# The last two down chunks in sets of 256 tokens, and a first transfer of 256 weight columns

## The reference, cut to what matters

```python
# start: layer 0 of the first block
h = rmsnorm(x, norm_g)                     # x (1, 512, 1024)
proj = jnp.einsum("bsd,de->bse", h, w_in)
...
# end: layer 1 of the second block
h = rms_norm(x, g_ffn[l])
x = x + jnp.square(jax.nn.relu(h @ w_ff1[l])) @ w_ff2[l]   # "up", then "down"
return rms_norm(x, g_final)
```

## Time and profile before

| | us |
|---|---|
| median of 3 runs | 1961.37 |
| the profiled execution, its own time | 1961.14 |
| its span | 1959.3 |
| TensorE busy | 1928.9 (98%) |
| VectorE busy | 1145.9 (58%) |
| GpSimd busy | 1013.0 (52%) |
| ScalarE busy | 768.7 (39%) |

### The profile page before, as it was taken

One profiled execution on the slowest core, in us unless ns is written; L12 is line 12 of the kernel. 1 busy time (PEld: TensorE's weight loads), 2 busy tenths in 40 slices (PEclk: granted clock), 3 DMA queues, 4 the chain that ended last, 5 costly groups with the idle time before them and its releaser, 6 DMA issues.

```text
span 1959.3 us, 24980 instructions
## 1 busy us (share of the span) xinstructions
PE 1928.9 (98%) x9110; PEld 1600.3 (82%) x9110; DVE 1145.9 (58%) x2009; ACT 768.7 (39%) x1142; POOL 1013.0 (52%) x1273
## 2 busy tenths in 40 slices
PE   9999999999999999999999999999999999999998
PEld 7788788888788887888888888888878888888887
DVE  7986778968867667463232325666676553332335
ACT  6444544445335455323232323344554233223232
POOL 6343374342733346665654646533447566464644
PEclk9999999999999999999999999999999999999999
DMA  5222222221321213222322232222222222323231
GB/s 200 80 76 75 69 93 88 83 85 50 113 86 65 86 65 108 99 96 86 114 86 108 86 108 86 86 86 87 86 75 98 99 96 86 108 86 108 86 108 65
DMA packets 29657, 178.92 MB, mean 91 GB/s; under 512 B 3936, under 2 KB 6112, under 8 KB 9184
## 3 DMA queue, kind: packets, MB, share of 16 engines
q1 hardware_dynamic: 27376, 173.42, 24.9%
q10 hardware_dynamic: 2160, 3.91, 0.7%
HBM read 175.22 MB, written 2.10 MB: 91 GB/s over the span
## 4 chain that ended last, share of the span: by engine, by line
PE 73%; DVE 14%; issue 6%; ACT 4%; POOL 2%; DMA 0%; SPq 0%; ACTq 0%; DVEq 0%; POOLq 0%
PE bank L584 67%; POOL W_lo L550 2%; PE bank L605 2%; DVE bank L1947 2%; DVE PR L1866 1%; DVE PT_lo L1759 1%; PE bank L635 1%; DVE Y_lo L1759 1%; ACT W_hi L1235 1%; PE bank L647 1%; ACT PR L1269 1%; ACT PT_hi L1239 1%; DVE PR L1887 1%; PE bank L846 1%; DVE K_lo L1759 0%
## 5 line engine op out<-in xcount | busy, mean ns | idle before, releaser
L550 POOL TENSOR_TENSOR W_lo<-W_raw,W_hi 128x256 fp32r<-128x256 f32 (+1 forms) x1228 | 986.9, 840 | 908.8 <-ACT W_hi L1235 908.8
L584 PE MATMUL bank<-H_hi,W_hi 128*128 128x512 f32 x1264 | 500.5, 396 | 2.8 <-POOL W_lo L550 1.0
L584 PE MATMUL bank<-H_hi,W_lo 128*128 128x512 f32 x1264 | 493.3, 390 | 0.0
L584 PE MATMUL bank<-H_lo,W_hi 128*128 128x512 f32 x1264 | 492.5, 390 | 0.0
L584 PE MATMUL bank<-Y_hi,W_hi 128*128 128x512 f32 (+1 forms) x980 | 384.9, 393 | 5.6 <-DVE Y_lo L1759 3.1
L584 PE MATMUL bank<-Y_hi,W_lo 128*128 128x512 f32 (+1 forms) x980 | 380.9, 389 | 0.0
L584 PE MATMUL bank<-Y_lo,W_hi 128*128 128x512 f32 (+1 forms) x980 | 380.7, 389 | 0.0
L1235 ACT ACTIVATE W_hi<-W_raw 128x2048 fp32r<-128x2048 f32 (+2 forms) x159 | 295.8, 1863 | 202.9 <-DMA W_raw<-in_stream 198.3
L584 PEld LDWEIGHTS bank<-H_hi,W_hi 128*128 128x128 f32 x1264 | 237.9, 188 | 52.0 <-DVE Y_lo L2329 1.8
L584 PEld LDWEIGHTS bank<-H_hi,W_lo 128*128 128x128 f32 x1264 | 237.5, 188 | 50.9
L584 PEld LDWEIGHTS bank<-H_lo,W_hi 128*128 128x128 f32 x1264 | 238.1, 188 | 47.4
(11 more groups left out here) (321 smaller groups left out, 2324.1 us busy)
## 6 DMA issues: line engine op xcount, KB each, us to landing
W_raw<-in_stream SPq DMA_DIRECT2D x159, 1024.0 KB, 4.8
out<-GT SPq DMA_DIRECT2D x8, 256.0 KB, 2.5
BT<-in_bias ACTq DMA_DIRECT2D x6, 320.0 KB, 3.0
X<-in_x SPq DMA_DIRECT2D x3, 512.0 KB, 7.5
W_raw<-in_stream SPq DMA_DIRECT2D x4, 256.0 KB, 7.2
BT<-in_rope ACTq DMA_DIRECT2D x2, 512.0 KB, 3.6
BT<-in_bias SPq DMA_DIRECT2D x2, 320.0 KB, 12.6
X<-in_x SPq DMA_DIRECT2D x2, 256.0 KB, 4.2
```

What stands on the lines that cost most here:

```text
L550: ins = nc.gpsimd.tensor_tensor(W[1][:, s, part], W_raw[:, s, part], W[0][:, s, part].bitcast(F32), ALU.subtract)
L584: mm = pe.matmul(out, lhs[a], rhs[b], start=(not begun and k == 0 and a == 0 and b == 0), stop=(not more and k == n - 1 and a == 1), skip_ ...
```

## The change

**At the end.** `down` now stops at d5 for PE and DVE. Chunks d6 and d7 are both done in sets of 256 tokens (`last_part`), in the order d6 set 0, d7 set 0, five of eight weight tiles of d6 set 1, the sums of set 0, the rest of d6 set 1, four tiles of d7 set 1, the spreads of set 0, the rest of d7 set 1, and then the sums and spreads of set 1. DVE handles each of the four pieces by `last_piece`, between them the inverse and two of the final multiplications of set 0. SP sends the piece of POOL second instead of fourth in set 0.

**At the start.** The weight pieces of unit 0 are now 256, 256, 512, 512 and 512 columns. The first of them goes out ahead of the gains and of X, and ACT makes its `W_hi` before it touches X.

The core of the diff:

```diff
+FIRST_PARTS = [slice(0, 256), slice(256, 512), slice(512, 1024), slice(1024, 1536), slice(1536, 2048)]
...
+    def half_bank(t, h):
+        return ((G[0], SC[0]), (G[1], TB[0]))[t - 6][h]
...
     @block.sync
+        first_weights(0)
         sp.dma_start(PARF[:, :], dram["gains"]).then_inc(gains_in, 16)
         sp.dma_start(X[:, 0, :], dram["x"][:, 0, :]).then_inc(x_first, 16)
-        for k in range(4):
...
+        first_weights(1)
+        sp.dma_start(X[:, 1, :], dram["x"][:, 1, :]).then_inc(x_in[0], 16)
+        for k in range(1, 4):
+            sp.dma_start(X[:, 2 * k:2 * k + 2, :], dram["x"][:, 2 * k:2 * k + 2, :]).then_inc(x_in[k], 16)
+            first_weights(k + 1)
...
-        for piece in ((0, 0), (0, 1), (0, 2), (0, 3), (1, 0), (1, 1), (1, 2), (1, 3)):
+        for piece in ((0, 0), (0, 3), (0, 1), (0, 2), (1, 0), (1, 1), (1, 2), (1, 3)):
...
     @block.gpsimd
-                    pool.wait_ge(w_half, kt // 2 + 1)
+                    pool.wait_ge(w_half, kt + 1 if kt < 2 else kt // 2 + 2)
...
     @block.tensor
-                    elif seg == "f3" and l + 1 == DEPTH and n == KT - 1:
-                        for h in range(2):
-                            part = [(w, [x[:, token_half(h)] for x in data]) for w, data in pairs]
-                            three(pe, (G[1], SC[0])[h][:, token_half(h)], part).then_inc(bf.half.sem, 1)
+                    elif seg == "f3" and l + 1 == DEPTH and n >= KT - 2:
+                        last_pairs.append(pairs)
...
+        def last_part(t, h, lo, hi):
+            part = [(w, [x[:, token_half(h)] for x in data]) for w, data in last_pairs[t - 6][lo:hi]]
+            mm = three(pe, half_bank(t, h)[:, token_half(h)], part, begun=lo > 0, more=hi < KT)
+            if hi == KT:
+                mm.then_inc(bf.half.sem, 1)
...
+        last_part(6, 0, 0, KT)
+        last_part(7, 0, 0, KT)
+        last_part(6, 1, 0, 5)
+        last_sums(0)
+        last_part(6, 1, 5, KT)
+        last_part(7, 1, 0, 4)
+        last_spreads(0)
+        last_part(7, 1, 4, KT)
+        last_sums(1)
+        last_spreads(1)
...
     @block.scalar
+        last_tile(6, 0)
         act.wait_ge(*own.last(0))
         nc.scalar.activation(spare_a[:, :], ones[:, 0:1], ACT.Sqrt).then_inc(act_step, own.step())
-        last_tile(0)
+        last_tile(7, 0)
         last_root(0)
-        last_tile(1)
+        last_tile(6, 1)
         copy_factors(0)
+        last_tile(7, 1)
         last_root(1)
         copy_factors(1)
...
     @block.vector
-                for n in range(KT - 1 if after and l + 1 == DEPTH else KT):
+                for n in range(KT - 2 if after and l + 1 == DEPTH else KT):
...
+        last_piece(6, 0)
+        last_piece(7, 0)
         last_inverse(0)
+        last_piece(6, 1)
         final_norm(0, 0)
+        last_piece(7, 1)
         final_norm(0, 1)
         last_inverse(1)
         final_norm(0, 2)
```

More of the change, by code:

```diff
@@ L227, in _build @@
     x_first = sem("x_first")
-    w_part = [sem(f"w_part{k}") for k in range(4)]
+    w_part = [sem(f"w_part{k}") for k in range(5)]
     start = sem("start")
@@ L342, in _build @@
     halves = ["0", "1"]
-    bf.half = Count(sem("last_half_done"), 0, [("", 1, halves)])
-    bf.x = Count(sem("last_half_added"), 0, [("", 1, halves)])
+    pieces = ["60", "70", "61", "71"]
+    bf.half = Count(sem("last_half_done"), 0, [("", 1, pieces)])
+    bf.x = Count(sem("last_half_added"), 0, [("", 1, pieces)])
     bf.sq = Count(sem("last_half_squares"), 0, [("", 1, halves)])
@@ L351, in _build @@
     bf.rs = Count(sem("norm_copiedF"), 0, [("", 1, halves)])
-    bf.xg = Count(sem("gain_times_xF"), 0, [("", 1, [str(k) for k in range(KT - 1)] + ["70", "71"])])
+    bf.xg = Count(sem("gain_times_xF"), 0, [("", 1, [str(k) for k in range(KT - 2)] + pieces)])
     final = Count(sem("final"), 0, [("", 1, ["00", "01", "02", "10", "11", "12"])])
@@ L500, in _, with first_weights @@
     def _(sp):
+        def first_weights(k):
+            part = FIRST_PARTS[k]
+            sp.dma_start(W_raw[:, 0, part], dram["stream"][0][:, part]).then_inc(w_part[k], 16)
+        first_weights(0)
         sp.dma_start(PARF[:, :], dram["gains"]).then_inc(gains_in, 16)
         sp.dma_start(X[:, 0, :], dram["x"][:, 0, :]).then_inc(x_first, 16)
-        for k in range(4):
[L504 to L509, removed]
+        first_weights(1)
[3 more added lines that the diff above has]
+            first_weights(k + 1)
         for n in range(1, UNITS):
@@ L1171, in up @@
                         pe_sums(pe, b2, l, "e", (ACC2,))
+            last_pairs = []
             def down(first, seg, i, last_up):
@@ L1202, in _, with last_sums @@
             down(58, "f3", 0, lambda count, n: count.at(l, f"u{n}", "f", 2))
-        for h in range(2):
+        def last_part(t, h, lo, hi):
[3 more added lines that the diff above has]
+                mm.then_inc(bf.half.sem, 1)
+        def last_sums(h):
             pe.wait_ge(bf.sq.sem, bf.sq.at(0, str(h)))
@@ L1298, in layer_params, with first_weights @@
                 .then_inc(ls_exp, own.reach(ls_exp, l + 1))
+        def first_weights(k):
+            part, signal = FIRST_PARTS[k], (w_half, k + 1) if k < 4 else (w_hi, 1)
+            act.wait_ge(w_part[k], 16)
+            act.wait_ge(*own.last(1))
+            nc.scalar.activation(W[0][:, 0, part], W_raw[:, 0, part], ACT.Copy).then_inc(signal[0], own.reach(*signal))
+        first_weights(0)
         act.wait_ge(gains_in, 16)
@@ L1307, in _ @@
             if k % 2 == 0:
[L1308 to L1312, removed]
+                first_weights(k // 2 + 1)
         for k in range(KT):
@@ L1712, in _ @@
         last_gain = GAINS["last"]
-        for k in range(KT - 1):
+        for k in range(KT - 2):
             act.wait_ge(b2.pre.sem, b2.pre.at(DEPTH - 1, f"x{k}", "f3"))
@@ L2665, in _, with last_piece @@
             down("f3", 0, True)
-        for h in range(2):
+        def last_piece(t, h):
             cols = token_half(h)
-            dve.wait_ge(bf.half.sem, bf.half.at(0, str(h)))
+            dve.wait_ge(bf.half.sem, bf.half.at(0, f"{t}{h}"))
             dve.wait_ge(*own.last(0))
-            nc.vector.tensor_tensor(PR[:, 1, cols], (G[1], SC[0])[h][:, cols], RB[:, cols], ALU.mult) \
+            nc.vector.tensor_tensor(PR[:, 1, cols], half_bank(t, h)[:, cols], RB[:, cols], ALU.mult) \
                 .then_inc(dve_step, own.step())
             dve.wait_ge(*own.last(0))
-            nc.vector.tensor_tensor(X[:, KT - 1, cols], X[:, KT - 1, cols], PR[:, 1, cols], ALU.add) \
-                .then_inc(bf.x.sem, own.event(bf.x, 0, str(h)))
+            nc.vector.tensor_tensor(X[:, t, cols], X[:, t, cols], PR[:, 1, cols], ALU.add) \
+                .then_inc(bf.x.sem, own.event(bf.x, 0, f"{t}{h}"))
             dve.wait_ge(*own.last(0))
-            nc.vector.tensor_tensor(PRE[:, 1, cols], X[:, KT - 1, cols], X[:, KT - 1, cols], ALU.mult) \
-                .then_inc(bf.sq.sem, own.event(bf.sq, 0, str(h)))
+            ins = nc.vector.tensor_tensor(PRE[:, 1, cols], X[:, t, cols], X[:, t, cols], ALU.mult)
+            if t == KT - 1:
+                ins.then_inc(bf.sq.sem, own.event(bf.sq, 0, str(h)))
+                return
+            ins.then_inc(dve_step, own.step())
+            dve.wait_ge(*own.last(0))
+            nc.vector.tensor_tensor(ACC2[:, cols], ACC2[:, cols], PRE[:, 1, cols], ALU.add) \
+                .then_inc(dve_step, own.step())
         def last_inverse(h):
```

11 lines of the change are left out of this document (6 added, 5 removed).

## The result

The changed kernel takes 1963.09 us, the median of 21 runs (1961.55 to 1966.48), against 1960.63 for the kernel before in as many (1958.92 to 1962.91). The ratio is 1.0012 with a 95% interval of 1.0006 to 1.0017: slower by 2.5 us (1.2 to 3.3 by the interval), a real loss, and under the 0.2% that the prediction called a difference. The forecast was 1962.1 us, 0.8 us slower than before, range 1960.8 to 1963.5.

The account below looks back on a forecast made before the run. TensorE, busy 1928.9 of 1959.3 us, was taken as the bound, so only the ends could move: +0.98 at the end and -0.2 at the start, +0.8 on 1961.14, plus 0.23 to the median: 1962.1 us, range 1960.8 to 1963.5.

Parts of the forecast that it names:

- The bound of the tail: End: norm and output queue both just about bind; set 1 arrives as the queue finishes set 0, in 11.2 us of tail.
- Products and inserts: End, TensorE: halves add 0.31 us, sums and spreads of set 0 0.90 each; last product +2.11 us.
- Where they begin: End, TensorE: products of d6 begin at 1936.91 as before, so the last product ends its issue at 1950.21.
- Do the inserts wait?: End: step checking whether sums and spreads of set 0 hold TensorE among the products; it claimed no wait for either.
- The sums of set 0: End: squares ready at 1944.21, 0.25 us before TensorE reaches these sums at 1944.46, so no wait.
- Case E: End, rival: sums of set 0 wait and hold the products by up to 0.7 us; time 1962.8, chance 0.06.
- The second set: End: sums of set 1 come 1.15 us late; with the output queue behind them the end is +0.98 us.
- case B: End, rival: spreads of set 1 run at full clock, end +0.47 us; time 1961.6, chance 0.28.
- The output queue: End: set 1's first data starts 0.92 us after issue, four pieces take 3.11 us; the queue ends last, at 1959.42.
- The start: Start: first product stays, last weight piece lands earlier; -0.2 us, bounds -0.3 and +0.4, carried through to the end.
- Case C: Start, rival: gain above 0.30 us because X tiles also land earlier; -0.9 us, time 1961.2, chance 0.12.
- Case D: Start, rival: clock falls in TensorE's gap after the first tile's products, slowing unit 0; time set at 1966, chance 0.04.

Follow-up runs that it names:

- e8: Kernel before, plus three unused matmuls on the tile of ones behind each set's sums; 1960.61 us against 1961.19, ratio 1.0000.
- e5: Kernel before, plus one wait of TensorE for DVE's scaling of d5 ahead of the products of d6; 1962.29 us against 1961.19, ratio 1.0007.
- e2: Changed kernel with the start of before, so only the end of the change; 1962.16 us against 1961.25 before, ratio 1.0009.
- e4: Only the end of the change, with the wait for d5's scaling moved between d6's and d7's first pieces; 1961.59 us against 1961.25 before, ratio 1.0004.
- e3: Changed kernel with the wait for d5's scaling moved between the first pieces of d6 and d7; 1961.94 us against 1961.25 before, ratio 1.0004.
- e7: Changed kernel with that wait moved, plus unused matmuls: six ahead of set 1's sums, three ahead of its spreads; 1961.91 us against 1961.19 before, ratio 1.0005.
- e9: Like e6, but SP sends POOL's piece of set 0 fourth, as before, instead of second; one execution, 1962.14 us.
- e1: Kernel before with only the start of the change (five weight pieces, the first ahead of the gains); 1961.8 us against 1961.25, ratio 1.0005.
- e10: The kernel of e1 unchanged, run again; 1961.84 us against 1960.92 before, ratio 1.0005.
- e6: Changed kernel with the wait moved and set 0's sums and spreads behind all products; 1962.82 us against 1961.19 before, ratio 1.0010.

## Why the prediction was right or wrong

**The bound of the tail: right.** Two chains were named, norm and output queue, that just about bind together. e8 takes 1 us from the spreads of set 1 and the tail does not move, so the queue is the one that ends last.

**Products and inserts: right.** 13.50 us forecast from the first product of d6 to d7 set 1 on DVE, 13.55 measured.

**Where they begin: wrong, and the largest miss.** "The last product ends its issue at 1936.91 + ..." took it for granted that d6 begins where it did. I had listed the waits of the new instructions (sums, spreads, second set) and not what became of the old ones when the products were moved out of a loop that kept its waits. The step "Do the inserts wait?" asked only about the inserts. The missing term is 1.13 us (e5) to 1.16 us (e2 less e4). It is larger than the whole forecast of 0.8 us, and no rival had it. The sentence on what would show it wrong did not name this place either.

**The sums of set 0: right.** No wait, although the margin was small: squares end at 1945.60, sums begin at 1945.86, so 0.26 us against 0.25 forecast. Case E fell, in every trace with the norm put among the products (after, e2, e3, e4, e7).

**The second set, +0.98 us, or +0.47 at full clock (case B): right in size for each clock, but not on when the clock falls.** With the wait out, e3, e4 and e7 have +0.38, +0.42 and +0.39 at full clock (e4 nearly so). At half clock, the changed kernel less 1.16 for the wait has +0.86; no trace shows this case without the wait. Which clock an execution gets is not a property of the kernel: the end of the change had half clock in one trace and full in two without any filling (e2, e3), nearly so in e4. Case B carried over from the trace of before that the clock falls 3.9 us behind the last product; it fell 2.7 us behind it in the changed kernel's trace and 5.2 in e3. Taking half clock as the likeliest was thin. For the kernel before the clock at these spreads costs nothing, as e8 shows. TensorE's idle of 1.4 us ahead of the sums, which I had held against case B, did not bring the clock down in e2 or e3. The Trainium skill (TensorE: Matmul & The Clock Gate, Part 1) has the moment of change move against the program from run to run; with 24.21 and 23.77 us for the same tail these traces agree.

**The output queue: right.** The fifth issue to the end took 4.84 us, 4.89 by the prediction's terms (0.92 + 3.11, and the 0.86 behind the data). That set 0 goes out early and gains nothing is what the DMA shares of 0.39 and 0.33 in the middle of the tail show. By the 2 us and bytes of the Trainium skill (DMA: Bandwidth & Descriptors, Anatomy of one DMA) the last issue would have counted; that section describes transfers issued by GpSimd, and these are issued by SP. e8 speaks against that rule here: its last issue is 0.46 us earlier than before, counted from d5's scaling, and its tail is the same to 0.03 us. From the last issue to the end it is 3.2 us before, 3.6 in e8, 3.0 after.

**The start, -0.2 us: undecided, and the step behind it too narrow.** The first product stayed (6.63 against 6.50), but the reason given for it does not hold: TensorE was through with the warming and idled 0.42 us for DVE in the trace after, and in e2 and e8, with the old start, 0.78 and 0.40 us for POOL's low tile. That all from unit 1 on hangs on ACT's copy of the last piece is right in eleven of twelve traces. Unit 1 starts 5.99 to 6.01 us after the copy in the six where ACT waited for that piece, and 6.13 to 6.18 in five others. But the bounds of -0.3 to +0.4 took two things for fixed: the landing, which lay anywhere from 14.04 to 15.43 with one and the same start, and that this landing is what ACT waits for, which was so in six traces only. The prediction had named a last landing more than half a microsecond from 14.0 as a sign of being wrong, and 14.74 in the trace after is one. In the profiled execution unit 1 started 0.69 us late, and d5 was 0.28 us late.

**The rivals at the start.** Case C (a gain above 0.30 us) is not shown in any run; its time of 1961.2 also lacks the 0.23 us between the profiled execution and the median, which the other cases add. Case D (the clock falls in the first gap) is not in the changed kernel's trace, where the granted clock is 1.00 up to 50 us. It does occur: in e9 the clock is 0.76, 0.50 and 0.89 in the three stretches of 2 us from 12 on. There TensorE comes to unit 1 without a wait, the only one of the twelve, and the sums behind it begin 10.87 us after the copy instead of 10.2 to 10.4. So a fall of some 3.4 us, estimated from those three stretches, cost about half a microsecond.

**The sum.** Wait 1.13 to 1.16, second set 0.4 at full and 0.86 at half clock: 1.6 us (e2) to 2.0 us (after), against 2.5 (1.2 to 3.3) by the runs; the 0.5 us between are within the interval and not explained. The direction held. Of the size, the forecast had a third, and the largest part of the loss was a term it did not have. That the measured 1963.09 lies in the range is luck: the range was laid around the median of three runs of the kernel before, 1961.37, which is 0.74 us above the median of 21. Around 1960.63 the same range would have ended at 1962.8.

## What to carry to other kernels

When instructions move, list the waits that stay behind as well as those that go along: an instruction taken out of a loop and issued after it inherits every wait of the loop's later turns, and neither the list of instructions nor a diff of them shows it. Before splitting work to feed an output queue early, check what ends last: here the queue was full either way from the last set's first piece on, and only that piece's time counted. When one trace gives a landing or a clock, it gives no bound on it. And when a copy starts, look whether its engine idled for the transfer or was itself late.

## What the runs showed of the hardware

The tail apart, executions differ ahead of it: DVE scales d5 between 1935.93 and 1938.58 in twelve traces, 2.65 us apart, although the instructions between the start and there are the same. Two sources are visible. One is the landing of the first transfers (1.4 us for the last weight piece with one start). The other is the granted clock in the attention stages, where TensorE is idle now and then. Stretches of the kernel before, and then of e1 (columns as in the earlier trace rows):

```profile
50.00:100.00 50.00, 46.82 (x221) 37.70 (x221) 44.87 (x82) 22.77 (x43) 15.01 (x21) 0.93 0.22 77
450.00:500.00 50.00, 47.25 (x243) 39.91 (x242) 40.55 (x92) 27.98 (x57) 20.19 (x25) 0.97 0.18 60
```
```profile
50.00:100.00 50.00, 46.76 (x234) 37.55 (x233) 45.79 (x83) 22.31 (x42) 15.26 (x21) 1.00 0.23 77
450.00:500.00 50.00, 47.30 (x242) 39.79 (x242) 40.58 (x91) 27.24 (x57) 21.00 (x26) 0.97 0.19 66
```

At 0.93 over 50 us the clock was at its lower level for 7 us of one execution and not at all in the other, with the same work. In other traces it fell elsewhere (0.97 in 150 to 200 us in the trace after, for one). How much of the spread of the runs (4 us before, 5 us after) comes from it was not tried.

A third source lies outside the span, and the yardstick does not see it. In every run with a recorded span of the kernels with the old end (before, e1, e5, e8, e10) the execution's own time is 1.75 to 1.87 us longer than its span. With the changed end it is now and then more: 4.18 us in the slowest run of the changed kernel (1966.48), 3.48 in one of e2, up to 3.29 in e4 and 2.89 in e6, and 1.76 to 2.30 in e3. The cause is open.
